# A fused decoder layer on one core: the first modulation blocks hold scale and shift together, and three input chunks are summed piece by piece behind them

## The reference

```python
mod = silu(c) @ ada_w + ada_b                      # ada_w: 2048 x 12288
sh1, sc1, g1, sh2, sc2, g2 = split(mod, 6)         # 2048 each
h = rms(x, norm1_g) * (1 + sc1) + sh1
z = h @ w_in          # 17 groups of 512 columns, and 20 narrow gate columns
y = concat(mlstm(z), moba(z), retention(z), nsa(z)) @ w_out
x = x + g1 * y
h2 = rms(x, norm2_g) * (1 + sc2) + sh2
out = x + g2 * hier_moe(h2)                        # 32 SwiGLU experts, top 2 of one group
```

## Time and profile before

| | |
|---|---|
| three runs, median (lowest, highest) | 1854.16 us (1849.34, 1855.04) |
| the profiled execution: its own time | 1856.19 us |
| its span, first to last instruction | 1854.4 us |
| mean granted TensorE clock, share of full speed | 0.886 |
| TensorE busy | 1408.7 us, 76% |
| VectorE busy | 422.7 us, 23% |
| ScalarE busy | 206.6 us, 11% |
| bytes moved | 613 MB, mean 331 GB/s |

### The profile page before, as it was taken

How to read it: one execution, slowest core, us unless ns; L and a number is a source line. 1 busy time by engine, 2 the same in 40 slices (tenths; PEclk the granted TensorE clock), 3 DMA queues, 4 the chain that set the end, 5 groups by cost and what they waited for, 6 DMA issues and landing times.

```text
span 1854.4 us, 28387 instructions
## 1 busy us (share of the span) xinstructions
PE 1408.7 (76%) x12911; PEld 880.4 (47%) x12911; DVE 422.7 (23%) x699; ACT 206.6 (11%) x424; POOL 32.7 (2%) x31
## 2 busy tenths in 40 slices
PE   2799999999999798997666566666665666666665
PEld 0467545585445674445353334443433434343443
DVE  0004343657354453002101001001010010100104
ACT  1100001101000010012101110111110101111011
POOL 0000000000000001002000000000000000000000
PEclk9888999999999899998887888778877888878787
DMA  8996576656864765332999999999999999999995
GB/s 311 386 374 239 196 283 248 272 229 236 317 234 179 313 245 215 139 143 92 410 427 420 422 426 392 427 421 417 427 398 428 424 415 427 416 418 426 389 428 215
DMA packets 48014, 613.03 MB, mean 331 GB/s; under 512 B 9096, under 2 KB 9776, under 8 KB 10128
## 3 DMA queue, kind: packets, MB, share of 16 engines
q1 hardware_dynamic: 41648, 601.97, 78.9%
q0 software_dynamic: 1088, 6.21, 0.9%
q10 hardware_dynamic: 5152, 2.85, 0.5%
HBM read 608.92 MB, written 2.10 MB: 329 GB/s over the span
## 4 chain that ended last, share of the span: by engine, by line
PE 52%; DMA 36%; DVE 6%; issue 3%; ACTq 2%; ACT 1%; POOL 0%; SPq 0%; DVEq 0%
DMA ring<-in_exp_w 32%; PE W L545 15%; PE W L537 8%; PE M L865 7%; PE W L793 6%; PE W L836 4%; DMA ring<-in_stream 4%; PE A L891 3%; PE W L824 2%; DVE ada_s L1206 2%; PE A L503 1%; DVE Z L1133 1%; ACTq L935 1%; PE A L520 1%; PE M L582 1%
## 5 line engine op out<-in xcount | busy, mean ns | idle before, releaser
L865 PE MATMUL M<-ring,Z 128*32 128x128 f32 x8192 | 321.5, 324 | 212.6 <-DMA ring<-in_exp_w 151.1
L865 PEld LDWEIGHTS M<-ring,Z 128*32 128x32 f32 x8192 | 279.5, 131 | 271.3 <-DMA ring<-in_exp_w 182.9
L545 PE MATMUL W<-ring,buf_h 128*128 128x512 f32 x768 | 333.7, 595 | 2.7 <-DMA ring<-in_stream 2.7
L545 PEld LDWEIGHTS W<-ring,buf_h 128*128 128x128 f32 x768 | 145.6, 191 | 183.1 <-issue 183.1
L891 PE MATMUL A<-ring,tmp 128*32 128x512 f32 x1024 | 157.8, 750 | 73.4 <-DMA ring<-in_exp_w 63.4
L1627 DVE SCALAR_TENSOR_TENSOR tmp<-tmp,M 128x128 f32<-128x128 f32 x32 | 9.2, 287 | 797.7 <-ACT tmp L1106 797.7
L537 PE MATMUL W<-buf_h,ring 128*128 128x256 f32 x768 | 177.9, 396 | 16.4 <-DMA ring<-in_stream 14.5
L1206 DVE SCALAR_TENSOR_TENSOR ada_s<-ring,small,ada_s 128x512 f32<-128x512 f32 x240 | 180.5, 752 | 8.5
L537 PEld LDWEIGHTS W<-buf_h,ring 128*128 128x128 f32 x768 | 152.7, 200 | 41.9 <-issue 17.5
L793 PE MATMUL W<-ring,buf_x 128*128 128x512 f32 x256 | 110.9, 593 | 1.2 <-ACT buf_x L1062 1.2
L891 PEld LDWEIGHTS A<-ring,tmp 128*32 128x32 f32 x1024 | 32.3, 123 | 166.8 <-DMA ring<-in_exp_w 95.2
(11 more groups left out here) (282 smaller groups left out, 661.2 us busy)
## 6 DMA issues: line engine op xcount, KB each, us to landing
ring<-in_exp_w SPq DMA_DIRECT2D x192, 2048.0 KB, 16.3
ring<-in_stream SPq DMA_DIRECT2D x94, 2048.0 KB, 8.6
buf_x<-in_x ACTq DMA_DIRECT2D x1, 2048.0 KB, 11.4
buf_h<-in_x POOLq DMA_DIRECT2D x1, 2048.0 KB, 13.1
out<-Z SPq DMA_DIRECT2D x2, 1024.0 KB, 3.9
g1b<-in_ada_b POOLq DMA_DIRECT2D x1, 1024.0 KB, 12.3
g2b<-in_ada_b POOLq DMA_DIRECT2D x1, 1024.0 KB, 16.5
consts<-in_consts POOLq DMA_DIRECT2D x1, 1024.0 KB, 18.5
```

Of the source, the lines that this page charges most:

```text
L545: ins = pe.matmul(W[:, o + tt * 512:o + tt * 512 + 512], hT[:, kk, tt * P:tt * P + P], w[:, 512 * k:512 * k + 512], start=(kk == 0), stop= ...
L865: ins = pe.matmul(M[32 * c:32 * c + 32, 512 * w13:512 * w13 + 128], XT[:, kk, 32 * q:32 * q + 32], w[:, 512 * k + 128 * c:512 * k + 128 * ...
```

## The change

1. **Paired modulation blocks.** The first eight ada blocks now hold 256 columns of sc1 and the same 256 of sh1. So each block completes two 128-wide tiles of h. Half 0 of each block is summed by VectorE (`ada_rows`, eight instructions), half 1 by TensorE (`ada_products`, now one half); VectorE adds the two (`ada_added`), and ScalarE's copy goes.
2. **Pieces of three chunks.** The weights of `n_kc`, `n_vc`, `n_q` are no longer six halves but eight "early" pieces of 1.5 MB (two tiles of each chunk). Piece n is multiplied behind block n: `n_kc` and `n_vc` (`early_turned`) behind it, `n_q` (`early_plain`) one block later, one part ahead of the block's combine and one after it. `n_q` accumulates in `M`. A piece's ring buffer is free (`early_used`) only after its `n_q` part. The last piece comes ahead of block 7's halves.
3. **A shorter `ORDER`.** It starts with `extras` and ada 8; `gates` and `cmp_hid` now stand behind `n_ks`, the later steps are shifted by a chunk up to `m_k`, ada 9 to 22 keep one a chunk, and ada 22 and 23 both stand behind `r_k`.
4. **The start.** One transfer brings all small vectors as columns, and `wx` and `w2c` come packed by the host: five transfers on ScalarE's queue instead of sixteen, none ahead of the stream on SP's. `turn_rows` and its copies go. GpSimd forms the mean, ScalarE scales x. `csil` holds one value and 31 zeros for each of eight tiles.

```diff
-ADA_FIRST = [4, 0, 5, 1, 6, 2, 7, 3]
+N_PAIRED = 8
 ADA_LATER = [16, 12, 17, 13, 18, 14, 19, 15, 8, 9, 10, 11, 20, 21, 22, 23]
-ORDER = [('chunk', 'n_kc'), ('extras', 0), ('ada', 8),
-         ('chunk', 'n_vc'), ('gates', 0),
-         ('chunk', 'n_q'), ('cmp_hid', 0), ('norm', 'n_q'), ('ada', 9),
-         ('chunk', 'n_ks'), ('cmp_out', 0), ('turn', 'n_q'), ('norm', 'n_ks'), ('ada', 10),
...
-         ('chunk', 'r_q'), ('turn', 'b_k'), ('scores', 'moba'), ('ada', 22),
-         ('chunk', 'r_k'), ('turn_p', 'moba'), ('ada', 23),
+EARLY = ('n_kc', 'n_vc', 'n_q')
+ORDER = [('extras', 0), ('ada', 8),
+         ('chunk', 'n_ks'), ('gates', 0), ('cmp_hid', 0), ('norm', 'n_q'), ('ada', 9),
+         ('chunk', 'n_vs'), ('cmp_out', 0), ('turn', 'n_q'), ('norm', 'n_ks'), ('ada', 10),
...
+         ('chunk', 'r_q'), ('turn', 'b_k'), ('scores', 'moba'), ('ada', 21),
+         ('chunk', 'r_k'), ('turn_p', 'moba'), ('ada', 22), ('ada', 23),
          ('chunk', 'r_g'), ('pv', 'moba'), ('r_scores', 0), ('turn_y', 'b'), ('r_pv', 0), ('turn_y', 'r')]
...
 def weight_stream():
+    items = []
+    for n in range(N_PAIRED):
+        if n == N_PAIRED - 1:
+            items.append(('early', n, 0))
+        items += [('ada', n, 0), ('ada', n, 1)]
+        if n < N_PAIRED - 1:
+            items.append(('early', n, 0))
...
 def by_vector(item):
-    return item[0] == 'ada' and item[1] >= len(ADA_FIRST)
+    return item[0] == 'ada' and (item[1] >= N_PAIRED or item[2] == 0)
...
                     if by_vector(STREAM[i - RING]):
                         sp.wait_ge(sem["ada_half_used"], dve_halves)
+                    elif STREAM[i - RING][0] == 'early':
+                        sp.wait_ge(sem["early_used"], early_halves)
                     else:
                         sp.wait_ge(half_used, pe_halves)
-                sp.dma_start(ring[i % RING][:], a['stream'][i]).then_inc(slot_full[i % RING], 16)
+                n = 3072 if kind == 'early' else HALF
+                sp.dma_start(ring[i % RING][:, 0:n], a['stream'][i][:, 0:n]).then_inc(slot_full[i % RING], 16)
...
+            for n in range(N_PAIRED):
+                if n == N_PAIRED - 1:
+                    half[0] += 1
                 ada_products(n)
+                if n > 0:
+                    w = ring[early_slot[n - 1] % RING]
+                    early_plain('n_q', n - 1, 0, w, 2048)
                 ada_combine(n)
+                if n > 0:
+                    early_plain('n_q', n - 1, 1, w, 2048).then_inc(sem["early_used"], 1)
+                else:
                     turn_x()
+                    pe.wait_ge(sem["xT_copied1"], 4)
+                i = early_slot[n]
+                w = ring[i % RING]
+                pe.wait_ge(slot_full[i % RING], 16 * (i // RING + 1))
+                pe.wait_ge(sem["h_ready"], n + 1)
+                early_turned('n_kc', n, w, 0)
+                early_turned('n_vc', n, w, 1024)
...
+            for n in range(N_PAIRED):
+                ada_rows(n, 0, n + 1)
+                item_done(dve, 'ada', n)
+                tt_op(ada_s[n % 2][:], ada_s[n % 2][:], A[:], ALU.add).then_inc(sem["ada_added"], 1)
+                dve.wait_ge(sem["ada_summed"], n + 1)
+                k0 = 2 * n
...
+                dve.wait_ge(sem["xT_copied1"], n // 2 + 1)
+                for k in range(k0, k0 + 2):
+                    ins = dve.tensor_scalar(hT[:, k, :], hT[:, k, :], gsc[:, k:k + 1], modc[:, KT + k:KT + k + 1],
+                                            ALU.mult, ALU.add)
+                ins.then_inc(sem["h_ready"], 1)
```

More of the change, by code:

```diff
@@ L55 @@
 NX = 2 * H + 3 * H
+N_COLS = 88 + 64 + 64 + 2
 CONST = {}
@@ L109, with part_of @@
 ORDER = place_sums(ORDER)
-CHUNKS = [a for s, a in ORDER if s == 'chunk']
+CHUNKS = list(EARLY) + [a for s, a in ORDER if s == 'chunk']
 MIX_Y = {'m': 0, 'b': 1, 'r': 2, 'n': 3}
-AFTER_ADA = {4: CHUNKS[0], 5: CHUNKS[1]}
+def part_of(n):
+    return ADA_LATER[n - N_PAIRED] // 4, ADA_LATER[n - N_PAIRED] % 4
 def weight_stream():
[L119 to L123, removed]
-    for step, arg in ORDER:
[L125 to L129, removed]
+    items = []
[5 more added lines that the diff above has]
+            items.append(('early', n, 0))
+    for step, arg in ORDER:
+        if step in ('chunk', 'ada', 'cmp_hid'):
+            items += [('cmp' if step == 'cmp_hid' else step, arg, 0), ('cmp' if step == 'cmp_hid' else step, arg, 1)]
+    return items + [('wout', n, hf) for n in range(D // 512) for hf in range(2)]
 STREAM = weight_stream()
@@ L139, in by_vector @@
 def by_vector(item):
-    return item[0] == 'ada' and item[1] >= len(ADA_FIRST)
+    return item[0] == 'ada' and (item[1] >= N_PAIRED or item[2] == 0)
 def halves_used(i):
     v = sum(by_vector(STREAM[j]) for j in range(i))
-    return i - v, v
+    e = sum(STREAM[j][0] == 'early' for j in range(i))
+    return i - v - e, v, e
 PE_BASE = halves_used(EXPERT_BASE)[0]
@@ new lines, in early_plain, with chunk_half @@
+            def early_plain(name, n, k, w, first):
+                dst = chunk_psum(name)
+                for tt in range(TT):
+                    kk = 2 * n + k
+                    ins = pe.matmul(dst[:, tt * 512:tt * 512 + 512], hT[:, kk, tt * P:tt * P + P],
+                                    w[:, first + 512 * k:first + 512 * k + 512], start=(kk == 0), stop=(kk == KT - 1))
+                return ins
+            def chunk_half(name, hf):
+                n = CHUNKS.index(name)
+                if hf == 0:
+                    pe.wait_ge(sem["chunk_copied"], {3: 1, 4: 2}.get(n, n - 1))
+                dst = chunk_psum(name)
@@ L531, in chunk_half @@
                 w = half_arrives()
-                if name in ('m_q', 'm_k', 'r_q', 'r_k', 'n_kc', 'n_vc'):
+                if name in ('m_q', 'm_k', 'r_q', 'r_k'):
                     for h in range(H):
@@ L1165, in ada_finish @@
             def ada_finish(n):
-                part, c = ADA[n] // 4, ADA[n] % 4
+                part, c = part_of(n)
                 dve.wait_ge(sem["ada_summed"], n + 1)
@@ L1677, in stream_half @@
     rows = slice(1024 * hf, 1024 * hf + 1024)
+    if kind == 'early':
+        tiles = slice(256 * arg, 256 * arg + 256)
+        parts = [rows_by_partition(inputs['w_in'][0, tiles, COL[n]:COL[n] + GW], 2) for n in EARLY]
+        return np.concatenate(parts + [np.zeros((P, HALF - 3072), np.float32)], 1)
+    if kind == 'ada' and arg < N_PAIRED:
+        w = np.asarray(inputs['ada_w'][0, rows])
+        return rows_by_partition(np.concatenate([w[:, D + 256 * arg:D + 256 * arg + 256],
+                                                 w[:, 256 * arg:256 * arg + 256]], 1), 8)
     if kind == 'ada':
-        return rows_by_partition(inputs['ada_w'][0, rows, 512 * ADA[arg]:512 * ADA[arg] + 512], 8)
+        o = 512 * ADA_LATER[arg - N_PAIRED]
+        return rows_by_partition(inputs['ada_w'][0, rows, o:o + 512], 8)
     if kind == 'chunk':
@@ L1699 @@
     arrays["in_consts"] = constants()
+    arrays["in_cols"] = columns(inputs)
+    w_in = np.asarray(inputs['w_in'][0])
+    arrays["in_wx"] = rows_by_partition(np.concatenate([w_in[:, COL['m_i']:COL['m_i'] + 2 * H],
+                                                        w_in[:, COL['n_g']:COL['n_g'] + 3 * H]], 1), KT)
+    arrays["in_w2c"] = np.concatenate([np.asarray(inputs['nsa_cmp_w2'][0, w]) for w in range(2)], 1)
     arrays["in_stream"] = np.stack([stream_half(inputs, *half) for half in STREAM])
```

319 lines of the change are left out of this document (145 added, 174 removed).

## The result

The changed kernel takes 1905.29 us (median of four runs, 1898.38 to 1913.82) against 1853.98 us: a ratio of 1.0284, 95% interval 1.0238 to 1.0329. It is 51 us slower. The forecast was 1882 us, 28 us slower, with a range up to 1902: the sign and most of the mechanisms held, and the amount is 23 us short. The profiled execution is the slowest of the four (1913.82 us, span 1912.0). A second profile of the same kernel, taken with later experiments (1905.24 us, span 1903.4), has the same waits, and I name it where a size differs.

A forecast was written before the change was run, and what follows sets the result against it. Early on the order of TensorE's work and its waits set the time, later the experts' weights. 12.7 us lost up to `cmp_hid` plus 15 before `r_g` made 28 later: 1882 us, range 1858 to 1902.

The forecast's parts named there:

- Part 1: From the kernel's start to the first freed piece: x lands at 12.2 us, that piece is used up at 42.9.
- T1: Moment at which the first early piece is used up and its buffer comes free, forecast at 42.9 us.
- Part 2: Ada blocks: the held piece delays the next halves; period 21.8 us, with 2.5 charged for each clock restart.
- T6: Moment in block 6 at which the previous block's piece is used up, forecast at 151.9 us.
- T7: Moment in block 7 at which the previous block's piece is used up, forecast at 177.4 us.
- Part 3: Behind the blocks, through `n_ks` and `cmp_hid`: a wait of 10.7 us, the end at 259.5, 12.7 us later than before.
- the mark: Moment with `n_ks` and `cmp_hid` both done: 246.8 us in the kernel before, forecast at 259.5.
- Part 4: Behind `r_k`, ada 22 and 23 together: `r_g` waits for a buffer, 13.1 us plus 2 for the clock, 15 later.
- (a): Rival for the blocks: TensorE's clock stays at its upper level, period 19.3 us, total 1865 us; chance 0.16.
- (b): Rival for the blocks: the clock stays low through the pieces too, period 24.5 to 25 us, total 1903; chance 0.12.
- (c): Rival: blocks run at the pace of work and bytes, 13.5 us, with halves in flight early; total 1824; chance 0.10.
- (d): Rival behind `r_k`: `r_g` does not wait, because VectorE gets to ada 22 earlier; total 1867 us; chance 0.09.

The follow-up runs named there:

- run 4: Changed kernel with x loaded from SP's queue, behind the first half of the stream, in place of ScalarE's: 1893.1 us.
- run 12: Changed kernel with x first on ScalarE's queue and two small loads of constants ahead of the stream on SP's: 1892.0 us.
- run 1: Changed kernel with `n_q`'s part of each piece multiplied right behind `n_kc` and `n_vc` in the same block, freeing the buffer there: 1879.0 us.
- run 3: Changed kernel with twelve unread products of 128x512 added on TensorE in the pause ahead of `cmp_hid`: 1893.4 us.
- run 9: Changed kernel with `n_q` at once, gates before `n_ks`, x behind the first half, ada 23 late, last piece behind block 7's halves, five filling products: 1839.9 us.
- run 5: Changed kernel with ada 23 moved to the end of the order, its sum behind `r_pv`: 1889.0 us.
- run 2: Changed kernel with `gates` ahead of `n_ks`, right behind `extras`: 1892.5 us.
- runs 11 and 12: The first is the changed kernel with x ahead of the small vectors on ScalarE's queue, 1903.2 us; the second is run 12.

## Why the prediction was right or wrong

**Part 1, the start: the step that failed first.** "x lands at 12.2 (0.8 + 11.4)" took x's 11.4 us over from the earlier trace rows and let only the stream come earlier. But x shares the transfer engines with the stream, and the change starts the stream 0.9 us sooner and x 0.4 us later. x landed at 22.34, and T1 came at 52.4, not 42.9. The constants landed at 28.3, and the first combine waited 8.3 us for them, under the wait for x. With x early T1 is at 44.9 (run 4) and 44.3 (run 12), so x is 7.5 to 8.1 of the 9.5 us. Run 12 shows that what stands first on the two queues decides when x lands, and runs 4 and 12 that it is worth 11 to 12 us at the end.

**Part 2, the blocks: right.** T6 - T1 is 157.8 - 52.4, a period of 21.1 us against 21.8. The wait is 5.8 us for 5.9. Two halves land 12.5 us after the piece is freed, for 12.7. T7 - T6 is 25.8 against 25.5. Run 1 shows that the held piece is the cause. Of 1.9 to 3.3 us for each restart the trace has 2.9 in block 2 and 1.8 in block 4 (the half block 3.64 for 1.85 in both, the first `n_q` part 3.06 and 1.91 for 1.91). The Trainium skill (TensorE: Matmul & The Clock Gate, HAM oscillation — how this bites in real kernels) describes tiles that each start cold, behind waits longer than their own work. "That is this block, by these rows" went too far: this block has 13.2 us of work and a wait of 5.8. But the cold start is in this trace: the half block behind each wait took 3.41 to 3.64 us for 1.85, so all or most of it ran at 1.2 GHz. The Trainium skill (DMA: Bandwidth & Descriptors, Anatomy of one DMA — SWDGE (gpsimd) path) gives its fit for transfers that GpSimd issues; by it the two halves would have landed after an estimated 11.6 us. They are issued by SP, and the trace has 12.5, so that figure was too short here.

**Part 3: the wait right, `cmp_hid` mis-sized.** The wait for the blocks is 10.7 us, as forecast. "`cmp_hid` 14.4, plus 1 to 2 for the clock" is the second step that failed: it measured 27.5. I had taken the clock's rise from chunks of 256 and 512 columns; the products here have 60. A row that could have warned me was in the chain: `extras`, 20 columns each, took 11.03 us. In the kernel before it began at the upper clock, and the clock fell while TensorE had no gap (stretches as in the earlier trace rows):

```profile
143.00:145.00 2.00, 2.00 (x15) 1.84 (x14) 0.00 (x0) 0.54 (x1) 0.00 (x0) 1.00 0.99 414
...
147.00:149.00 2.00, 2.00 (x11) 2.00 (x11) 0.00 (x0) 0.00 (x0) 0.00 (x0) 0.50 0.95 410
```

It stayed at 0.50 to the end of `extras`. Run 3 shows for `cmp_hid` that the pause ahead of it is the cause, and run 9 shows it again behind a pause of 3.8 us. With `n_ks` 30.07 for 29.4, the mark stood at 279.1, 32.3 us late, not 12.7: 6.2 from the start less the blocks, 1.4 in front of `n_ks`, 0.7 in it, and 11.5 in `cmp_hid`; that is the missing 20.

**Part 4: right in kind, 5 to 7 us short.** `r_g` starts 17.5 us after the end of `r_k` in this profile (15.5 in the second), where I had 15.7; it takes 30.1 to 30.6 for 27.7. The two sums of ada 22 and 23 now stand one behind the other ahead of `pv`, 2.0 us more, for which the forecast has no term. From the end of `r_k` to the first output chunk the kernel before took 45.4 us and this one 67.9 (65.4 in the second profile): 20 to 22.5 us for the 15. Undoing it (run 5) wins 15 to 16 us by the medians; its trace has 47.4 us for this stretch.

**The sum.** The start's gain was 9.5 us smaller, and the clock in `cmp_hid` cost 11.5 more. Corrected for these two, 28 becomes 49, and 51 was measured. That this fits so closely is partly luck. The blocks took 3.3 us less than forecast, part 4 took 5 to 7 more, and between the mark and the end of `r_k` another 3.7 us came up (3.3 in the second profile), for which the forecast has no term and whose cause stays open. In the two profiles the first output chunk starts 58.5 and 53.9 us later than before (787.95 and 783.32 against 729.45), and what is behind it takes 1124.1 and 1120.1 us, where it took 1125.0.

**The rivals.** (a) and (b) did not come: in each block the clock fell in the pause or right behind it, and rose again. The measured time is next to (b)'s 1903 by coincidence: the period was 21.1, not 24.5. (c) did not, but it was the right lever: run 1 is its mechanism at a period of 17.1, not 13.5. (d) did not.

## What to carry to other kernels

In a ring that is filled strictly in order, ask of every buffer how long it is held after it has landed, not how busy the engines are: one piece held for one block made 13.2 us of work last 21. When narrow products stand behind a pause, look at what such products did to the clock elsewhere in the trace; here they took the lower clock for their whole length, and wide work in the pause paid for itself. Read a list of waits one by one, since the longest of them may be the first of the kernel; and when transfers are reordered at a kernel's start, don't carry a landing time over from the old profile. And test the parts of a change alone: here the smallest part was the gain, and the rest hid it.

## What the runs showed of the hardware

- Products of 128x128 weights and 60 columns ran 27 us without a gap at a granted clock of 0.50 (the changed kernel), and 14 us at 1.00 when wide products ran just ahead (run 3).
- Products of 20 columns began at 1.00 and were at 0.50 some 3 us later, without a gap (`extras` in the kernel before, 144 to 149 us).
- Behind a pause of 3.8 us the clock fell from 1.00 to 0.50 as the products of 60 columns began (run 2).
- A 2 MB load on ScalarE's queue took 21.2, 17.5 or 7.9 us from issue to landing beside the same stream on SP's queue; the three differ in what stands first on the two queues (the changed kernel, runs 11 and 12).
